# One more expert matrix held in memory, a reordered attention stage, short POOL instructions and an output written by column halves

## What is computed

```python
h = rmsnorm(x, g_mix[l])
(cq, ckv, kr, aq, ak, av, qi, ki, wi, rq, rk, rv, rg) = jnp.split(h @ w_in[l], split_at, axis=-1)
...
x = x + jnp.concatenate([o_a, o_b, o_c], axis=-1) @ w_out[l]       # latent, sparse, retention
x = x + jnp.square(jax.nn.relu(rmsnorm(x, g_mlp[l]) @ w_ff1[l])) @ w_ff2[l]
...
# last step of the second block: 32 experts, two per row, D_EXPERT = 512
hid = jax.nn.silu(xb @ w_expert_gate[e]) * (xb @ w_expert_up[e])
y = hid @ w_expert_down[e]                                        # times the row's gate, summed over its experts
x = x + y
```

## Time and profile before

| | us |
|---|---|
| median of 3 runs | 1525.53 (1520.87 to 1526.18) |
| the profiled execution, its own time | 1522.61 |
| its span, first to last instruction | 1520.5 |
| TensorE busy | 1465.9 (96%) |
| VectorE busy | 712.9 (47%) |
| ScalarE busy | 544.9 (36%) |
| POOL busy | 416.8 (27%) |

### The profile page before, as it was taken

The page is one execution under the profiler, slowest core; times in us unless marked ns, Lnnn a source line. Parts: engine busy times, 40 slices in busy tenths (PEclk is TensorE's granted clock), DMA queues, the critical chain, the costliest instruction groups (busy, mean ns, idle before and its releaser), DMA issues.

```text
span 1520.5 us, 19911 instructions
## 1 busy us (share of the span) xinstructions
PE 1465.9 (96%) x7762; PEld 1047.2 (69%) x7762; DVE 712.9 (47%) x1076; ACT 544.9 (36%) x812; POOL 416.8 (27%) x153
## 2 busy tenths in 40 slices
PE   8998999999998999999999999998999899999997
PEld 7887888887787888887787679855454344454442
DVE  6665475575675475664158644734112111112111
ACT  6555543345656543334455421112111111111111
POOL 2462443434362334345858220100000000000000
PEclk9999999999999999999999999999999999999999
DMA  6341356554341354556764601027899999999995
GB/s 265 133 152 56 123 183 202 186 190 165 125 159 56 107 196 169 202 186 224 222 242 138 236 22 39 1 111 332 339 427 428 428 428 428 424 424 418 429 428 233
DMA packets 44417, 351.81 MB, mean 231 GB/s; under 512 B 5187, under 2 KB 7151, under 8 KB 19759
## 3 DMA queue, kind: packets, MB, share of 16 engines
q1 hardware_dynamic: 43502, 349.35, 59.9%
q10 hardware_dynamic: 720, 1.14, 0.2%
q0 software_dynamic: 112, 0.17, 0.1%
HBM read 347.71 MB, written 1.07 MB: 229 GB/s over the span
## 4 chain that ended last, share of the span: by engine, by line
PE 71%; DMA 10%; DVE 7%; issue 6%; DVEq 2%; ACT 2%; POOL 2%; POOLq 0%; SPq 0%; ACTq 0%
PE psum L1701 12%; PE psum L1040 9%; PE psum L1042 9%; PE psum L1041 9%; DMA ring<-in_w_expert_up 9%; PE psum L1316 8%; PE psum L1728 5%; PE psum L1318 4%; PE psum L1030 3%; PE psum L1660 2%; PE psum L1669 1%; PE psum L1126 1%; POOL weights_split L886 1%; PE psum L1145 1%; PE psum L1531 1%
## 5 line engine op out<-in xcount | busy, mean ns | idle before, releaser
L886 POOL TENSOR_TENSOR weights_split<-weights_raw,weights_split 128x2048 fp32r<-128x2048 f32 (+4 forms) x101 | 361.0, 3592 | 414.6 <-ACT weights_split L1802 414.6
L1802 ACT ACTIVATE weights_split<-weights_raw 128x2048 fp32r<-128x2048 f32 (+4 forms) x154 | 243.4, 1586 | 237.8 <-PE psum L1042 138.5
L1701 PE MATMUL psum<-ring,arena 128*64 128x512 f32 x976 | 225.9, 597 | 13.4 <-DMA ring<-in_w_expert_up 12.2
L1316 PE MATMUL psum<-h_split,weights_split 128*128 128x512 f32 x512 | 181.2, 397 | 1.4 <-DVE weights_split L886 1.4
L1701 PEld LDWEIGHTS psum<-ring,arena 128*64 128x64 f32 x976 | 73.6, 138 | 148.5 <-issue 148.4
L1040 PE MATMUL psum<-weights_split,h_split 128*128 128x512 f32 (+3 forms) x400 | 153.3, 383 | 4.6 <-POOL weights_split L886 2.9
L1040 PE MATMUL psum<-weights_split,hidden_split 128*128 128x512 f32 (+1 forms) x384 | 151.2, 394 | 5.2 <-DVE hidden_split L1790 5.2
L1042 PE MATMUL psum<-weights_split,h_split 128*128 128x512 f32 (+3 forms) x400 | 151.0, 378 | 0.0
L1041 PE MATMUL psum<-weights_split,h_split 128*128 128x512 f32 (+3 forms) x400 | 150.9, 377 | 0.0
L1042 PE MATMUL psum<-weights_split,hidden_split 128*128 128x512 f32 (+1 forms) x384 | 149.2, 389 | 0.0
L1041 PE MATMUL psum<-weights_split,hidden_split 128*128 128x512 f32 (+1 forms) x384 | 148.9, 388 | 0.0
(11 more groups left out here) (376 smaller groups left out, 2033.6 us busy)
## 6 DMA issues: line engine op xcount, KB each, us to landing
weights_raw<-in_layer_w SPq DMA_DIRECT2D x94, 1024.0 KB, 4.8
arena<-in_w_expert_down SPq DMA_DIRECT2D x32, 2048.0 KB, 13.4
ring<-in_w_expert_up SPq DMA_DIRECT2D x32, 2048.0 KB, 17.0
ring<-in_w_expert_gate SPq DMA_DIRECT2D x29, 2048.0 KB, 16.2
weights_raw<-in_second_w SPq DMA_DIRECT2D x44, 512.0 KB, 4.9
arena<-in_w_expert_gate SPq DMA_DIRECT2D x3, 2048.0 KB, 9.8
weights_raw<-in_layer_w SPq DMA_DIRECT2D x6, 768.0 KB, 4.1
ring<-in_w_out SPq DMA_DIRECT2D x2, 2048.0 KB, 17.0
```

The lines of the kernel that those rows point to most:

```text
L886: eng.tensor_tensor(W.part(j, 1, n), W.raw(j, n), W.part(j, 0, n).bitcast(F32), ALU.subtract).then_inc(W.lo[W.pieces[j][1]], 1)
L1316: pe.matmul(both.rearrange("p (w s) -> p w s", w=2), w[0][:, k, f * P:(f + 1) * P], hTp[:, :, k, :], start=(k == 0), stop=False)
L1701: ins = pe.matmul(bank[half(j), :], xe[h][:, k, half(j)], w[j][:, k, :], start=(k == 0), stop=(k == KD - 1))
L1802: act.activation(W.part(j, 0, w), W.raw(j, w), ACT.Copy).then_inc(W.hi, 1)
```

## The change

Five edits:

1. A tenth expert matrix, the first gate matrix of turn 14, is held. It lies over the rows x and the front of the tables, so its load waits for the last "rank" unit and for the normalised rows; the table "incl" is moved behind the overlaid part and a gap of 126 columns added.
2. The accumulators start with identity times x, and the sum with x at the end is gone. In the last turn the give-back of the turn before stands between gate and up.
3. The end goes by column halves: give-back of one half, VectorE and ScalarE copy a row half each, one store per half.
4. POOL's low-part subtraction in the first block goes in steps of 512 columns, but for the pieces of the first input block.
5. In the attention the retention scores stand ahead of the sparse scores and take four banks; VectorE empties them before the sparse maxima, and normalises retention before it takes sparse results 2 and 3; mixed units 2 and 3 are turned, and split by ScalarE and VectorE, ahead of the dense loop.

```diff
+LOW_STEP = 512
...
-    plan += [scores[0], scores[1]] + interleave("retS", len(RET_UNITS), (6, 7), "V")
+    plan += interleave("retS", len(RET_UNITS), (6, 7, 4, 5), "V")
...
-    plan += uq[:T] + [ret_out[0], turned[0], turned[1], ret_out[1]] + uq[T:]
+    plan += [scores[0], scores[1], ret_out[0]] + uq[:T] + [turned[0], turned[1], ret_out[1]] + uq[T:]
...
-    plan += [("mlaT", 4 + j, j, "A") for j in range(4)]
+    plan += [("mlaT", 4 + j, j, "A") for j in range(4)] + mix[2:]
...
-RESIDENT = {(TURNS // 2, 0): 0, (TURNS // 2 + 2, 0): 1, (TURNS // 2 + 4, 0): 2}
+RESIDENT = {(TURNS // 2, 0): 0, (TURNS // 2 + 2, 0): 1, (TURNS // 2 + 4, 0): 2, (TURNS // 2 + 6, 0): 3}
...
-            eng.tensor_tensor(W.part(j, 1, n), W.raw(j, n), W.part(j, 0, n).bitcast(F32),
-                              ALU.subtract).then_inc(W.lo[W.pieces[j][1]], 1)
+            eng_name = W.pieces[j][1]
+            step = LOW_STEP if W is LW and eng_name == "P" and W.pieces[j][0][:2] != ("in", 0) else n
+            for c in range(0, n, step):
+                cols = slice(c, min(c + step, n))
+                ins = eng.tensor_tensor(W.part(j, 1, n)[:, cols], W.raw(j, n)[:, cols], W.part(j, 0, n).bitcast(F32)[:, cols], ALU.subtract)
+            ins.then_inc(W.lo[eng_name], 1)
...
-                     (5, ("yrw", 2 * T - 1)), ("R", 0, ("mixT", 3)), (2, SW.last[2]), (3, SW.last[3])]
+                     (5, ("yrw", 2 * T - 1)), ("R", 0, ("mixT", 3)), (2, SW.last[2]), (3, SW.last[3]),
+                     ("R", 3, ("rank", T))]
...
                 project_q(0, 1)
-                units.wait_emptied(*(("dsaT", t) for t in range(T)))
-                mask_ready.wait(pe, 1, l)
-                attend_scores(0)
-                attend_scores(1)
-                project_q(1, 0)
-                project_q(1, 1)
                 units.wait_emptied(*(("retT", t) for t in range(T)))
                 for i, (t, s, h0) in enumerate(RET_UNITS):
...
-                project_q(2, 0)
+                project_q(1, 0)
+                units.wait_emptied(*(("dsaT", t) for t in range(T)))
+                mask_ready.wait(pe, 1, l)
+                attend_scores(0)
+                attend_scores(1)
+                project_q(1, 1)
...
                 retention_out(0)
+                project_q(2, 0)
...
+                units.wait_emptied(("O", 2), ("O", 3))
+                turn_mix(2)
+                ret_ready.wait(pe, 1, l)
+                turn_mix(3)

                 for g in range(N_DSA, NG + 2):
...
-                pe.matmul(final.bank(("acc", u)), zeros, second("levels")[:, 0:512], start=True, stop=False)
+                pe.matmul(final.bank(("acc", u)), ident, x[:, u // 2, u % 2 * 512:(u % 2 + 1) * 512], start=True, stop=False)
...
+                    if last and stage == "up":
+                        give_rows_before()
...
-            units.wait_emptied(("y", 1, 1))
-            give_back(last=True)
+            for c in range(2):
+                units.wait_emptied(("y", 1, c))
+                give_back((c,), last=True)
...
+            final = UnitView(FU, act, psum)
+            for c in range(2):
+                bank = final.wait_full(("acc", 2 + c))
+                final.emptied_by(("acc", 2 + c), act.activation(y_out[:, 1, c * 512:(c + 1) * 512], bank, ACT.Copy), "A")
```

More of the change, by code:

```diff
@@ L549, in shape_tables @@
     c["flip"] = np.eye(P)[::-1]
+    c["gap"] = np.zeros((P, 126))
     c["places"] = np.tile(np.arange(SLOTS_E), (P, 1))
@@ L556 @@
 FIRST = ("cos32", "sin32", "cos64", "sin64", "decay")
-SECOND = ("cum_incl", "cum_excl", "halves", "minus_strict", "incl", "minus_level1", "level1T", "levels",
-          "bucket_hot", "flip", "places", "rank")
+SECOND = ("cum_incl", "cum_excl", "halves", "minus_strict", "minus_level1", "level1T", "levels",
+          "bucket_hot", "flip", "gap", "incl", "places", "rank")
 ROWS, _at = {}, 0
@@ L838, in program @@
         moe_loaded = [sem(f"moe_loaded{s}") for s in range(MOE_SLOTS)]
-        resident_loaded = [sem(f"resident_loaded{j}") for j in range(3)]
-        moe_done = sem("moe_done")
+        resident_loaded = [sem(f"resident_loaded{j}") for j in range(4)]
         fills_ready = sem("fills_ready")
@@ L963, in _ @@
                 units.wait_full(load[-1])
+                if load == ("R", 3, ("rank", T)):
+                    sp.wait_ge(xn2_ready, 1)
                 if load[0] == "R":
@@ L993, in _ @@
                     sp.dma_start(dst, src).then_inc(moe_loaded[s], 16)
-            for t in range(T):
-                sp.wait_ge(moe_done, t + 1)
-                sp.dma_start(out[0, t * P:(t + 1) * P, :], x[:, t, :]).then_inc(out_stored, 16)
-            sp.wait_ge(out_stored, 16 * T)
+            stored = UnitView(FU, sp, psum)
+            for c in range(2):
+                stored.wait_emptied(*(("acc", 2 * t + c) for t in range(T)))
+                cols = slice(c * 512, (c + 1) * 512)
+                sp.dma_start(out[0].rearrange("(t p) d -> p t d", p=P)[:, :, cols], y_out[:, :, cols]).then_inc(out_stored, 16)
+            sp.wait_ge(out_stored, 32)
         def bridge(pe, units, key, n):
@@ L1275, in _ @@
                     n = g - N_DSA
-                    if n == 0:
-                        units.wait_emptied(("O", 2), ("O", 3))
-                        turn_mix(2)
-                        ret_ready.wait(pe, 1, l)
-                        turn_mix(3)
                     if n == 1:
@@ L1650, in _ @@
             for _ in range(4):
-                pe.matmul(psum[:, 7, 0:256], ident, second("levels")[:, 0:256], start=True, stop=True)
+                pe.matmul(psum[:, 7, 0:256], ident, shared("causal")[:, 0:256], start=True, stop=True)
             units.wait_emptied(*(("rank", i) for i in range(T + 1)))
@@ L1662, in gather, with give_back @@
                 return ins
-            def give_back(last=False):
-                for u in range(2 * T):
-                    t, c = u // 2, u % 2
-                    for part in range(2):
-                        ins = pe.matmul(final.bank(("acc", u)), takeT[:, t * P:(t + 1) * P], y_parts[:, part, c * 512:(c + 1) * 512],
-                                        start=False, stop=(last and part == 1))
-                    if last:
-                        final.finish(("acc", u), ins)
+            def give_back(halves_, last=False):
+                for c in halves_:
+                    for t in range(T):
+                        for part in range(2):
+                            ins = pe.matmul(final.bank(("acc", 2 * t + c)), takeT[:, t * P:(t + 1) * P], y_parts[:, part, c * 512:(c + 1) * 512],
+                                            start=False, stop=(last and part == 1))
+                        if last:
+                            final.finish(("acc", 2 * t + c), ins)
             pe.wait_ge(xn2_ready, 1)
@@ L1712, in turn @@
                 ins.then_inc(EU.full, 3 if last else 1)
-                units.wait_emptied(("gt", 1 - h), 1 - h)
-                units.wait_emptied(("y", 1 - h, 1), 1 - h)
-                give_back()
+                if not last:
+                    give_rows_before()
                 bank = units.begin(("gt", h))
@@ L2917, in _ @@
             final = UnitView(FU, dve, psum)
[L2918 to L2925 removed]
+            for c in range(2):
+                bank = final.wait_full(("acc", c))
+                final.emptied_by(("acc", c), dve.tensor_copy(y_out[:, 0, c * 512:(c + 1) * 512], bank), "V")
 def kernel(**inputs):
```

42 lines of the change are left out of this document (19 added, 23 removed).

## The result

The changed kernel took 1500.42 us (median of four runs, 1493.93 to 1510.0) where the kernel before took 1523.22 (four, 1520.87 to 1526.18). The ratio is 0.986, with an interval of 0.983 to 0.988: 1.4% faster. The forecast was 1507, with a range of 1500 to 1517. The profiled execution took 1502.05 us with a span of 1500.2, so 20.3 us less than the 1520.5 of before (the medians differ by 22.8); the forecast in these terms was 18.8. The total came out; its parts did not.

What follows compares the result with a forecast made beforehand. Bounds: TensorE work in feed-forward, TensorE's waits and lowered clock in attention, DMA in the experts. Attention -12.0 and experts with tail -6.8 gave -18.8 from 1525.53, so 1507 us; own range 1501 to 1513, wider 1500 to 1517.

Steps and rivals of the forecast that it cites:

- Tenth matrix and give-back: Expert turns 14 and 15: loads land 4.9 us earlier, the moved give-back saves more; last down 5.1 us sooner.
- Tail: End of the kernel: give-back and copies by halves take 1.8 us in place of 3.5, so -1.7 us.
- the stores: Final stores, half-rows of 2 KB in place of whole rows: same bytes, so cost taken as 0.
- Mix rows ahead: Attention, turned mix rows ahead of dense scores: first turned dense probabilities 5.5 us sooner in layer 0, 6.2 in layer 1.
- wait for exponentials: Attention, dense part after the reorder: ScalarE's exponentials are what comes late next, by 0.6 us.
- with short waits: Attention: VectorE normalises retention by 123.0 with short waits, so the mix rows' copies end by 126.5.
- Retention ahead: Attention, retention units before sparse scores: fifth unit stalls about 2.4 us; -0.1 us in layer 0, -0.9 in layer 1.
- Short POOL pieces: First block, POOL's pieces cut to 512 columns: mask ends at 90.5 for 94.94, index scores +0.5 us per layer.
- alternation: Index scores: POOL takes turns with VectorE, so a chain waits once per short piece: +0.5 us per layer.
- (a): Rival: attention gain mostly lost to retention stalls and exponentials, +1 in place of -12; 1520 or 1513 us; chance 0.27.
- (b): Rival: TensorE alone holds turns 14 and 15, so the held matrix gains nothing; 1510.5 us; chance 0.06.
- (c): Rival: short pieces make POOL the pace of the first block's feed-forward; slower, 1542 us; chance 0.03.

Runs made afterwards that it cites:

- retention_behind_again: The changed kernel with the retention units behind the sparse scores again, all else kept: 1498.98 us, ratio 0.983.
- core_filler: The changed kernel with three spare matmuls in TensorE's 0.78 us wait ahead of the core's right-hand sides in the second block: 1497.03 us, ratio 0.982.
- mix_rows_alone: The kernel before with only the turned mix rows moved ahead of the dense scores, POOL's pieces left long: 1521.81 us, ratio 1.000.
- pieces_of_256: The changed kernel with POOL's pieces at 256 columns in place of 512: 1491.01 us, ratio 0.978.
- without_tenth_matrix: The changed kernel without the tenth resident matrix, so turn 14 loads all six again: 1501.13 us, ratio 0.986.

## Why the prediction was right, and where it was not

**Tenth matrix and give-back: right.** Forecast -5.1, measured -4.75 (442.65 to 437.90 us from first turn to last down). Turn 15's up came 3.1 us sooner, forecast 3.2. For the moved give-back the words say that 1.3 us are left, but the sum takes the whole 1.87; from the up to the down it was 1.6 (11.08 became 9.46). No DMA wait is left at the ups of turns 14 and 15, as foretold, and the load lies in the empty stretch. The bound given for it ("if all of the wait stayed it would be -1.3") was too good: without the matrix the give-back's move is worth 0.1.

**Tail: right in kind, -1.2 for -1.7.** From the last down's start to the end 15.2 became 14.0. From the last y emptied (1494.79) to the last word copied it was 1.9 us, forecast 1.8:

```profile
1496.08 0.60 ACT L2152 ACTIVATE arena<-psum 128x512 f32<-128x512 f32 x1 [1.05 <-PE psum L1680]
```

The mis-sized term is the stores, taken as 0: they end 3.5 us behind the last copy, 3.1 before, so the half rows cost 0.4.

**Mix rows ahead: right in kind, the size partly luck, on a condition that the prediction named only in passing.** Short pieces alone bring the first turned dense probabilities of layer 0 to 133.06, with the new order 127.82: -5.2 for -5.5. But this is both parts of the order and the clock. With the mix rows ahead and retention in its old place (retention_behind_again) they are at 130.77, so -2.3; at full clock, -3.1 (130.6 to 127.5). The wait for exponentials that was foretold at 0.6 us is 0.67 and 0.70, and no stall stands between the dense scores and the first out-projection. Without short pieces the time gains nothing. The step said "with short waits"; it did not say that the same reorder with long ones puts a second 4.8 us instruction ahead of the bank that the queries need.

**Retention ahead: the edit is worth nothing, as forecast (-0.1, -0.9),** though this part ended 3.6 us earlier (99.65 for 103.24). Short pieces alone have it at 99.41. The stall at the fifth unit was forecast at 2.4 us with half clock behind it; it was 1.17 with the clock kept (in core_filler, with the same wait of 1.15, it wasn't: 0.84 from 90 to 101 us). The mask ended at 88.3, forecast 90.5, because its last two instructions began at 85.8 for 88.1: the index scores ahead of them had ended sooner.

**Short POOL pieces: the step that failed.** It said of the index scores "nearest is alternation: +0.5 per layer". Up to the first turned dense probabilities of layer 0 the sum had +0.5 - 0.1 - 5.5 = -5.1; measured was -10.95, of which short pieces alone give -5.7 (138.77 to 133.06). Two things are in this.

First, alternation is real, but it was worked out the wrong way. Five VectorE instructions stand in a row against four short pieces. The first four each ended with a piece (1.00, 1.23, 1.21 and 1.21 us), the fifth ran free (0.35), and the last ended at 55.00 where it had ended at 55.61. So ScalarE's second read-back came 0.6 us sooner and not 0.6 later, and its first one 2.3 us sooner.

```profile
49.67 1.00 DVE L2287 TENSOR_SCALAR arena<-arena,stat 128x128 f32<-128x128 f32 x1 [4.55 <-ACT arena L1864]
50.75 4.25 DVE L2291 SCALAR_TENSOR_TENSOR arena<-arena,stat 128x128 f32<-128x128 f32 x4
```

Second, the clock. TensorE's matmuls there took 2.00 us before because they stood in the middle for the second read-back; the granted clock was still 1.00, and it fell in the projection behind them (0.50 from 57.7 to 59 us). Of the 2.2 us by which the turned latent rows come sooner (72.57 for 74.78), 0.6 is the read-back and 1.6 this low clock. It follows long pieces in three of four profiles (mix_rows_alone is the exception) and short ones, 1024 columns and less, in none of ten; that it will always stay away is not shown. At full clock layer 0 gained 4.8 us up to the first turned dense probabilities (132.6 to 127.8), 2.0 of them by short pieces alone (130.6). The forecast of -5.1 is near that by luck: it came from +0.5 and -5.6, where at full clock it was -2.0 and -2.8.

The Trainium skill ("SBUF — State Buffer", section on the two separate sides) says that a VectorE instruction in a mode that uses both ports contends with GpSimd, and so does one with two SBUF inputs if the GpSimd instruction reads SBUF; whichever starts first holds the shared ports for its whole instruction and blocks the other. The runs agree: the first index instruction, held by one piece, took 4.32, 2.11, 1.00 and 0.46 us with pieces of 2048, 1024, 512 and 256 columns. The use made of it against this change, that four short pieces block as long as one long one, held only in chains. The prediction's "4.31 us for 0.29 us of work" pairs two instructions: the 4.31 is the mask's last, of 256 columns, which takes 0.42 or 0.44 where no piece holds it (layer 1 of mix_rows_alone, pieces_of_256).

**The clock: the term that was missing on both sides.** The prediction charged low clock behind each remaining wait. In the profile after, no stretch of layer 0 is under 1.00 (of layer 1 one, 0.89 from 422 to 438), and attention gave 22.4 us, not 12, about 14 of them low clock. And it had no term for a clock that falls elsewhere, from a cause that no run shows; in the profiled run that was 6.5 us. That the shorter waits are what keeps the clock up in attention is likely, for the runs of before have mean clocks of 0.984 to 0.991 and the eight of the change 0.989 to 0.998; but in no run were the waits alone varied. The two errors nearly cancel: the total is right partly by luck. Of the rivals, (a) fell, since attention gained nearly twice the forecast; (b) fell by the 4.6 us of without_tenth_matrix; (c) fell: POOL's busy time grew from 416.8 to 448.5 us and no feed-forward matmul waits for it.

## What to carry to other kernels

Where two engines lock each other out, the length of the other engine's instruction is the latency of yours: cut it before reordering around it, and test the two together, for here the order alone cost 12 us, the cut alone gave 10, and all parts together 17 more than their sum (at full clock 4, 4 and 9). When the clock can fall, read span times clock beside the span: it was steady to 0.35% where the spans differed by 1.2%, and it shows that of the 21 us of this change 13 are code and 8 are clock. A wait can be removed by putting ready work into it: two such moves gave 5 us of code.

## What was not expected of the hardware

A wait of 1.17 us at the fifth retention unit left the clock at 1.00, and one of 0.19 us at the index scores of before was followed by half clock. Nor does the same place always do the same: core_filler has the first wait (1.15 us) with a lower clock behind it, mix_rows_alone the second without one. The length of the wait alone does not say whether the clock falls. The same matmuls with the same wait (0.78 us ahead of the core) ran on at 2.4 GHz in nine profiles and at 1.2 GHz for some 13 us in three. In attention a VectorE instruction that reads two SBUF operands takes up to about as long as the POOL piece that it meets: 4.8, 2.7, 1.6 and 1.1 us for pieces of 2048, 1024, 512 and 256 columns (4.65, 2.4, 1.3 and 0.74 us). POOL is held up as well: five pieces of 512 columns took 7.28 us beside the rotation and the normalisation, four took 4.98 where VectorE had few such instructions.
